# A two-block fp32 model on one core: the matrix products of the identity taken out of TensorE's order of work

## The reference

```python
def hybrid_layer(x, ...):                      # first block, 2 layers
    u = rms_norm(x, attn_norm_w) @ w_in
    mix = concatenate([hgrn2_mixer(...), dilated_attention_mixer(...), mamba2_mixer(...)])
    x = x + mix @ w_out
    x = x + peer_ffn(rms_norm(x, ffn_norm_w), peer_w_query, peer_sub_keys, peer_down, peer_up)

def second_block(x, mem, ...):                 # 2 layers, then a final norm
    h = rmsnorm(x, norm_mix[l]);  p = h @ w_in[l]
    merged = g_a * y_a + g_b * y_b + g_c * y_c # convolution, retention, spatial gating
    x = x + merged @ w_o[l]
    x = x + cross_attention(rmsnorm(x, norm_xa[l]), rmsnorm(mem, norm_mem[l]), ...)
    h = rmsnorm(x, norm_ffn[l])
    x = x + (silu(h @ w1[l]) * (h @ w3[l])) @ w2[l]
```

## Time and profile before

| | us |
|---|---|
| median of 3 runs | 3047.66 |
| lowest and highest | 3045.5 and 3049.07 |
| the profiled execution, its device time | 3047.16 |
| its span, first to last instruction | 3045.4 |
| TensorE busy in the span | 2959.6 |
| mean granted TensorE clock | 0.989 of full |

### The profile page before, as it was taken

One profiled execution on the slowest core, in us unless ns is written; L12 is line 12 of the kernel. 1 busy time (PEld: TensorE's weight loads), 2 busy tenths in 40 slices (PEclk: granted clock), 3 DMA queues, 4 the chain that ended last, 5 costly groups with the idle time before them and its releaser, 6 DMA issues.

```text
span 3045.4 us, 43973 instructions
## 1 busy us (share of the span) xinstructions
PE 2959.6 (97%) x17364; PEld 2615.8 (86%) x17364; DVE 2030.2 (67%) x3055; ACT 1447.7 (48%) x2254; POOL 14.9 (0%) x37
## 2 busy tenths in 40 slices
PE   8899999999999898999999999999999999999998
PEld 6788888889999877888888999988898998888996
DVE  5759998765555586699886555557565556665554
ACT  5431575454444444237645444435555444545443
POOL 0000000000000000000000000000000000000000
PEclk9999999999999999999999999999999999999999
DMA  5334455776455432345568545546555666554563
GB/s 176 90 102 154 151 180 199 235 259 218 169 202 180 135 105 97 139 141 174 196 208 285 217 175 196 190 156 176 177 174 168 190 188 182 172 184 144 149 187 124
DMA packets 223246, 528.52 MB, mean 174 GB/s; under 512 B 13450, under 2 KB 87344, under 8 KB 212080
## 3 DMA queue, kind: packets, MB, share of 16 engines
q1 hardware_dynamic: 221856, 521.11, 51.9%
q0 software_dynamic: 1232, 5.25, 0.5%
HBM read 507.42 MB, written 18.88 MB: 173 GB/s over the span
## 4 chain that ended last, share of the span: by engine, by line
PE 88%; DVE 9%; ACT 2%; issue 1%; DMA 0%; SPq 0%; ACTq 0%; POOL 0%; DVEq 0%; POOLq 0%
PE ps L2169 15%; PE ps L2153 12%; PE ps L1260 12%; PE ps L1273 11%; PE ps L1244 11%; PE ps L1210 9%; PE ps L556 4%; PE ps L547 4%; PE ps L1199 2%; PE ps L2410 1%; PE ps L644 1%; DVE arena L1722 1%; DVE arena L1714 1%; DVE arena L1712 1%; DVE arena L1771 1%; DVE arena L1768 1%
## 5 line engine op out<-in xcount | busy, mean ns | idle before, releaser
L1827 DVE TENSOR_TENSOR ring_lo<-ring,w_hi 128x1024 fp32r<-128x1024 f32 x320 | 388.4, 1224 | 270.2 <-ACT w_hi L1823 269.1
L1210 PE MATMUL ps<-h_t,ring 128*128 128x256 f32 x2048 | 466.6, 381 | 0.9 <-ACT arena L869 0.9
L1823 ACT ACTIVATE w_hi<-ring 128x1024 fp32r<-128x1024 f32 x320 | 336.7, 1057 | 268.5 <-PE ps L2169 181.8
L1210 PEld LDWEIGHTS ps<-h_t,ring 128*128 128x128 f32 x2048 | 381.4, 191 | 48.5 <-issue 1.3
L1260 PE MATMUL ps<-h_t_lo,down_hi 128*128 128x256 f32 x1024 | 288.2, 281 | 0.0
L1260 PE MATMUL ps<-h_t_expert,down_lo 128*128 128x256 f32 x1024 | 287.8, 281 | 0.0
L1260 PE MATMUL ps<-h_t_expert,down_hi 128*128 128x256 f32 x1024 | 286.8, 280 | 0.0
L2153 PE MATMUL ps<-h_t_hi,w_hi 128*128 128x256 f32 x928 | 259.9, 280 | 2.7 <-ACT arena L1968 2.7
L2153 PE MATMUL ps<-h_t_lo,w_hi 128*128 128x256 f32 x928 | 261.4, 282 | 0.0
L2153 PE MATMUL ps<-h_t_hi,ring_lo 128*128 128x256 f32 x928 | 259.7, 280 | 0.0
L1631 DVE TENSOR_TENSOR up_lo<-ring,up_hi 128x2048 fp32r<-128x2048 f32 x64 | 146.7, 2292 | 97.9 <-ACT up_hi L925 97.9
(11 more groups left out here) (438 smaller groups left out, 6727.8 us busy)
## 6 DMA issues: line engine op xcount, KB each, us to landing
ring<-in_peer_down SPq DMA_DIRECT2D x128, 1024.0 KB, 5.0
ring<-in_w_in SPq DMA_DIRECT2D x140, 512.0 KB, 3.6
ring<-in_peer_up SPq DMA_DIRECT2D x68, 1024.0 KB, 4.8
ring<-in_w SPq DMA_DIRECT2D x132, 512.0 KB, 3.7
ring<-in_peer_up SPq DMA_DIRECT2D x120, 512.0 KB, 4.3
arena<-late_gates SPq DMA_DIRECT2D x16, 1024.0 KB, 6.4
ring<-in_w_out SPq DMA_DIRECT2D x16, 512.0 KB, 3.5
ring<-in_peer_w_query SPq DMA_DIRECT2D x16, 512.0 KB, 3.5
```

The lines of the kernel that those rows point to most:

```text
L1210: m = pe.e.matmul(PS[:, act_bank(b), j * T:(j + 1) * T], RING[:, b % 2, j * D + kc * P:j * D + (kc + 1) * P], HT[:, kc, :], start=kc == 0, ...
L1823: a.e.activation(W_HI[:, g % HI_SLOTS, :], RAW[:, g % RAW_SLOTS, :], ACT.Copy).then_inc(*a.count(f"c{g}_hi"))
L1827: v.e.tensor_tensor(RAW_LO[:, g % RAW_SLOTS, :], RAW[:, g % RAW_SLOTS, :], W_HI[:, g % HI_SLOTS, :].bitcast(F32), ALU.subtract).then_inc(* ...
```

## The change

All 137 dummy products go: 2 x (16 + 7 + 11 + 7) in the first block and 20 + 8 + 18 + 9 in the second. The helper `spin` and the argument `turns` go with them. Nothing else is altered, no wait and no other instruction, and the order of the rest stays.

```diff
-        def spin(pe, n, bank):
-
-            for _ in range(n):
-                pe.e.matmul(PS[:, bank, 0:T], IDENT, COMMON[:, 0:T], start=True, stop=True)
-
-        def turn_tensor(pe, tag, src, nk, ready, free=(), turns=0):
+        def turn_tensor(pe, tag, src, nk, ready, free=()):
 
             for name in free:
                 pe.e.wait_ge(*pe.at(name))
-            spin(pe, turns, 7)
...
-            turn_tensor(pe, "n1", SCR, KD, ["n1_xn0", "n1_xn1"], ["hybrid_start"], 16)
+            turn_tensor(pe, "n1", SCR, KD, ["n1_xn0", "n1_xn1"], ["hybrid_start"])
...
             pe.e.wait_ge(*pe.at("h7_ev"))
-            spin(pe, 7, 3)
             pe.e.wait_ge(*pe.at("dec_bc"))
...
-            turn_tensor(pe, "mx", MIX, KD, ["mix", "mix"], turns=11)
+            turn_tensor(pe, "mx", MIX, KD, ["mix", "mix"])
...
-            spin(pe, 7, 7)
             norm_turn(pe, "n2", (4, 6))
...
                 if l == 0:
                     wait("hybrid_end")
-                    spin(pe, 20, 3)
                     norm_turn(pe, "nx0", NX_BANKS)
-                    spin(pe, 8, 3)
...
                 else:
-                    spin(pe, 18, 2)
                     norm_turn(pe, "nf1", NF_BANKS, ["xo12_l", "xo13_l"])
-                    spin(pe, 9, 2)
```

## The result

| | before | without the dummies |
|---|---|---|
| median, us | 3047.79 | 3058.9 |
| lowest and highest of 11 runs | 3045.5, 3051.55 | 3054.4, 3060.84 |
| span of the profiled execution | 3045.4 | 3058.6 |
| mean granted TensorE clock | 0.989 | 0.976 |

The ratio is 1.0033, with a 95% interval of 1.0025 to 1.0042. So taking 60 us of useless work off TensorE made the kernel slower, by 7.6 to 12.8 us. The prediction said 3047 and gave 12% to slower; the time is outside its range.

The account below looks back on a forecast made before the run. TensorE was taken to bound the kernel, holding 88% of the chain of waits. The terms, 0 - 4.4 + 3.0 + 0.7 - 1.4 + 0 + 1.6 = -0.5, took 3047.16 to 3046.7, said as 3047 us; range 3042 to 3054.

Parts of the forecast that it names:

- B: Wait for the decays ahead of the state-space products, both layers: clock falls without the 7 dummies, +1.5 us twice, +3.0.
- A: First turn of each layer, while VectorE still splits weights: transposes at half are hidden, products already at half, 0 us.
- D: Turn at the residual's norm in each layer: products at full behind the transposes, layer 1 losing its half-clock stretch, -1.4 us.
- C: Turn of `MIX` in each layer: transposes at half cost +2.2, layer 0's half-clock stretch goes for -1.5, together +0.7 us.
- 129.01: Time in the trace before: products at full pace behind 18 slow transposes, taken as evidence that transposes bring the clock back.
- E: Second-block turn with 20 and 8 dummies: products start 1.3 us sooner, then lose 1.3 at half clock, 0 us.
- F: Second-block turn with 18 and 9 dummies: scaling and products start sooner, -4.4 us.
- let one fail for 1.6: Allowance of +1.6 us for one of five turns at C, D and F where transposes fail to bring the clock back.
- The slower one: Rival: transposes do not hold the clock, products at C, D and F start at half, 3053 to 3057; 16%.
- The gain of F: Rival that it is absorbed: products starting 4.4 us earlier meet an unsplit or unlanded chunk further down, 3051.1; 10%.
- The faster one: Rival: the clock hardly falls, gains at E, F, C of layer 0 and D of layer 1 total 8.8 us, 3038.4; 6%.

## Why the prediction was wrong, step by step

**B, predicted +3.0, measured 7.2 to 7.4 in the traces, and 10.9 for the site alone.** This is the step that failed, the larger of two. I took it that the clock falls there, and it does. But I let it stay low for "some 3.4 us", the length of the stretches at half behind A and D, and scaled the slowdown from transposes. Those stretches had products of 256 and 512 columns running when they ended. The state-space products have 64 columns each, and while they run the clock does not rise: 7.70 us of them at 0.50. The upper bound, 6, with all of them at half, was the right case, and still low, because the ratio is not 0.212 to 0.123, that of the transposes, but 7.70 (36 records) to 4.25 (37). I should have asked of each stretch at half what was running when it ended. The earlier trace rows have wide products or 18 transposes behind every rise, and none has products of 64 columns.

**C, predicted +0.7 for both layers, measured 1.3 in layer 0 and 2.9 in layer 1.** The transposes do run at half (3.56 us, 3.4 predicted), and the products are late by 1.3, 1.1 predicted. The transposes also bring the clock back, as taken from 129.01: it is at 1.00 for the last of them and for the first products (177.20 to 178.50). What failed is the last part, the second failed step: that the clock, once back, would hold for the products. The gap of 1.90 us between transposes and products, which I thought too short to matter, is all the idleness between that rise and the fall 1.3 us into the products, and the stretch at half is there after all.

The Trainium skill, page "TensorE: Matmul & The Clock Gate", section on PE-mode transpose, says that the full clock does not engage for transposes. At C of the changed kernel it did: the clock is at 1.00 in 175.15:175.35, while the last of them run. At E and F it did not, with 16 transposes at half each time (3.64 and 3.65 us). The experiments do not say what makes the difference.

**D, predicted -1.4, measured +1.6.** Layer 0 went from full to half, where I had both layers at full. The step that failed is that the transposes would run at half and bring the clock back. They started at full behind 3.51 us of idleness, the clock fell 1.3 us into them (1.00 in 204.57:205.80, 0.50 in 205.90:207.00), and the few that were left, 2.51 us for all 16, did not raise it. So the fall came ahead of the gap of 1.87 us behind them, and not from it. In layer 1, where I had a gain of 1.6, it went the same way and the stretch at half stayed. Of the five turns at C, D and F where I assumed products at full, and let one fail for 1.6, none kept the clock.

**E, predicted 0.** The gain of 1.3 is 1.2. The loss was taken as 1.3 and is 2.7 by the count of products (2.5 by the table), since they stayed at half for 5.9 us. **F, predicted -4.4.** The gain is 4.0, and the stretch at half behind it, which stood in the bounds only, takes 1.9. Alone, by the medians: +2.3 and -2.6, neither clear of nothing.

**A, predicted 0.** It was tested with C and D only. In the two traces nothing changes across A of layer 1 (its first product is 5.6 us later, and products 70 us behind it are 5.5 later), and it is under 1 us in layer 0.

**The rivals.** The slower one, with 3053 to 3057 and more, was the right side, and its place at C, D and F was partly right; its main place, B, was in no rival. The gain of F was not absorbed. The faster one, that the clock hardly falls, is out: 14 dummies alone make 11 us. In the terms of the sum, B at its measured size adds 4.4 us to the forecast; by itself that would have left the time in the range. It is out of it because C adds 3.5, D 3.0, E 1.5 and F 2.3 as well, of which the 1.6 set aside for one failed turn covers only a part: -0.5 + 4.4 + 10.3 - 1.6 = 12.6. With 1.5 at the wait of 1.93 us and 1.1 less ahead of B in layer 0 that is 13.0 of the 13.2 us between the two traces.

What stays open: by the median B alone costs 10.9 us where the products show 7.2, and the parts sum to 13.2 where the whole is 11.1. Which turns fall beside those of the edited site differs between profiles: D of layer 0 at full before, at half without B's dummies; the wait of 1.93 us at full in five profiles and at half in nine. One such turn is 1.5 us, so these remainders have the size of one or two such turns, but I have not separated them.

## What to carry to other kernels

Before taking work off an engine because nothing waits for it, read the granted clock of what comes behind it. Look behind the gap and not only in it: here the clock fell up to 1.3 us after work had started again. What a stretch at half costs depends on the instructions behind the gap: 1.6 to 2.7 us here where they were wide products, and the slower pace of the whole run, 3.7 us at B, where they were narrow. Dummies belong in the gaps, as many as the gap holds: at B three instead of seven let the clock fall, and at E and F the surplus delayed the turn. They are not any instruction that keeps the engine busy: with 6 rows instead of 128 they held nothing and cost 56 us. And compare several profiles before giving a microsecond or two to a cause, because here the clock fell behind the same wait of 1.93 us in some and not in others.

## What the runs showed of the hardware

- Being busy does not hold the clock. Dummies of 6 rows kept TensorE busy for 3.25 of 3.50 us and the clock fell; 22 of their records took 9.6 us at 0.50 with no rise.
- Products of 128x64 ran for 7.7 us at 0.50 without a rise; seven products of 128x256 put among them brought it to 1.00 within 4.8 us.
- Products of 64 columns keep pace with the clock too: 4.25 us at 1.00, 7.70 at 0.50.
- Idle gaps of 1.9 us can be enough. At C of the changed kernel one of 1.90 us was followed by half clock 1.3 us into the products, and one of 1.93 us in the second block was followed by half clock in nine of 14 profiles and by full clock in five. One of 2.29 us ahead of narrow products cost nearly as much as one of 3.7: 3057.1 us against 3058.2.
- The clock can fall after work has started again: 1.3 us into the transposes of D behind 3.51 us of idleness, over 0.3 us into the state-space products behind 3.69, where B's dummies stood in their middle.
- The clock can rise while transposes run: at C of the changed kernel, 0.50 in 171.82:175.10 and 1.00 in 175.15:175.35. At E, 16 transposes left it at half.
